# Norm sums in column strips, inverse roots spread by row groups: one change to a hybrid decoder kernel

## The reference

```
z = einsum('btd,dn->btn', h, w_in)                       # one projection, 88 tiles of 128 columns
q = rms_norm(a_q, a_q_norm) * 64 ** -0.5                 # attention, 3 groups x 8 heads x 64
k = rms_norm(a_k, a_k_norm)
o_b = rms_norm(o_b, b_out_norm) * silu(b_g)              # gated linear attention (GLA), 4 heads x 128
cq = l2_norm(cq) * 128 ** -0.5;  ck = l2_norm(ck)        # gated DeltaNet, 4 heads x 128
o_c = rms_norm(o_c, c_out_norm) * silu(c_z)

def rms_norm(x, w): return x * rsqrt(mean(x * x) + 1e-6) * w
def l2_norm(x):     return x * rsqrt(sum(x * x) + 1e-6)
```

## Time and profile before

| | |
|---|---|
| median of 3 runs | 1831.47 us (1829.76 to 1833.31) |
| profiled execution | 1828.83 us, span 1826.8 us |
| TensorE busy | 1749.6 us, 96% |
| VectorE, ScalarE, GpSimd busy | 746.2 (41%), 362.8 (20%), 154.7 us (8%) |
| chain that ended last | PE 85%, DMA 7%, SP's queue 3%, DVE 2% |

### The profile page before, as it was taken

One profiled execution on the slowest core, in us unless ns is written; L12 is line 12 of the kernel. 1 busy time (PEld: TensorE's weight loads), 2 busy tenths in 40 slices (PEclk: granted clock), 3 DMA queues, 4 the chain that ended last, 5 costly groups with the idle time before them and its releaser, 6 DMA issues.

```text
span 1826.8 us, 30009 instructions
## 1 busy us (share of the span) xinstructions
PE 1749.6 (96%) x12509; PEld 1289.6 (71%) x12509; DVE 746.2 (41%) x1549; ACT 362.8 (20%) x760; POOL 154.7 (8%) x259
## 2 busy tenths in 40 slices
PE   8999999999999999999999998999979989999987
PEld 5888888787768999978898887866844343333434
DVE  3444542434536676443635314273243222233222
ACT  2141333323101000013213343231010100100001
POOL 3000000403200111000100001041000000000000
PEclk9999999999999999999999999999989999999999
DMA  9833599999999997899527899899658999999993
GB/s 270 288 121 110 178 326 318 357 318 353 384 348 388 374 324 271 307 352 369 160 77 264 285 349 340 314 375 380 220 209 311 393 378 414 387 398 393 380 415 150
DMA packets 263163, 563.94 MB, mean 309 GB/s; under 512 B 11965, under 2 KB 160673, under 8 KB 262752
## 3 DMA queue, kind: packets, MB, share of 16 engines
q1 hardware_dynamic: 243696, 500.14, 75.8%
q0 software_dynamic: 18544, 58.58, 9.2%
q10 hardware_dynamic: 784, 3.25, 0.5%
HBM read 547.74 MB, written 196.63 MB: 407 GB/s over the span
## 4 chain that ended last, share of the span: by engine, by line
PE 85%; DMA 7%; SPq 3%; DVE 2%; issue 1%; ACT 1%; POOL 0%; ACTq 0%; DVEq 0%; POOLq 0%
PE PS L929 34%; PE PS L1580 7%; PE PS L1361 7%; PE PS L1337 4%; PE PS L1369 4%; PE PS L850 3%; SPq L804 3%; PE PS L1351 3%; PE PS L1618 3%; DMA mem<-in_moe_w_up 3%; PE PS L973 3%; PE PS L1560 3%; DMA z<-in_moe_w_down 2%; PE PS L966 2%; PE PS L1521 2%
## 5 line engine op out<-in xcount | busy, mean ns | idle before, releaser
L929 PE MATMUL PS<-h,mem 128*128 128x264 f32 x2816 | 655.2, 389 | 0.0
L929 PEld LDWEIGHTS PS<-h,mem 128*128 128x128 f32 x2816 | 528.5, 191 | 107.0 <-issue 21.3
L1763 ACT COPY z<-PS 128x264 f32<-128x264 f32 (+6 forms) x311 | 127.6, 431 | 817.3 <-PE PS L929 528.4
L1580 PE MATMUL PS<-mem,z 128*32 128x512 f32 (+1 forms) x1536 | 150.4, 536 | 12.4 <-DMA mem<-in_moe_w_up 5.8
L1580 PEld LDWEIGHTS PS<-mem,z 128*32 128x32 f32 x1536 | 52.9, 113 | 87.4 <-issue 77.1
L2841 DVE COPY small<-mem 128x1024 f32 x56 | 38.9, 694 | 171.8 <-PE PS L1560 109.4
L1560 PE MATMUL PS<-small,z 128*32 128x256 f32 (+2 forms) x624 | 87.8, 396 | 0.0
L1337 PE MATMUL PS<-z,mem 128*128 128x264 f32 x384 | 87.3, 388 | 0.0
L1560 PE MATMUL PS<-z 128*32 128x256 f32 (+2 forms) x624 | 87.0, 396 | 0.0
L1337 PEld LDWEIGHTS PS<-z,mem 128*128 128x128 f32 x384 | 72.3, 190 | 13.8 <-issue 1.7
L1361 PE MATMUL PS<-z,mem 128*128 128x132 f32 x624 | 77.4, 276 | 0.0
(11 more groups left out here) (364 smaller groups left out, 2018.9 us busy)
## 6 DMA issues: line engine op xcount, KB each, us to landing
out_win_s<-in_cache_win_kv SPq DMA_DIRECT2D x128, 1023.5 KB, 11.6
mem<-in_w_in SPq DMA_DIRECT2D x88, 1024.0 KB, 7.4
mem<-in_moe_w_gate SPq DMA_DIRECT2D x40, 1024.0 KB, 12.7
mem<-in_moe_w_up SPq DMA_DIRECT2D x40, 1024.0 KB, 12.6
mem<-in_moe_w_down SPq DMA_DIRECT2D x32, 1024.0 KB, 15.6
out_win_s<-in_cache_win_kv SPq DMA_DIRECT2D x32, 1022.0 KB, 12.4
z<-in_moe_w_down SPq DMA_DIRECT2D x24, 1024.0 KB, 14.2
z<-in_moe_w_up SPq DMA_DIRECT2D x16, 1024.0 KB, 13.7
```

The costliest lines, as they stand in the source:

```text
L929: last = mm(bank(l, "p", j)[:, 0:T], w[:, k, P * (j % 2):P * (j % 2) + P], h[:, k, :], start=(k == 0), stop=(k == KT - 1))
L1580: last = mm(m_bank("c", "gu", g, b, w, r)[BLK * j:BLK * j + BLK, 0:n], hs[:, k, P * r + BLK * j:P * r + BLK * j + BLK], v3(slot_ap(set_slo ...
L1763: return nc.scalar.copy(out, in_)
```

## The change

`norm_sum` on TensorE becomes four products of 32 columns: `K(...)[:, 48:80]`, the 32 columns of the matrix that straddle its middle, against one tile of squares each, written to four strips of 32 partitions of one bank, `n1`. So the sums of tile t lie in rows 32t to 32t + 31; with `blk` the first 16 of them are those of the head's lower half, the others those of the upper. ScalarE takes one logarithm and one exponential over that bank, 264 columns. A new step `norm_out` spreads the result: four products of 32 rows (row group t) with the constant `spread`, which picks row 0 of the group for the output's partitions 0 to 63 and row 16 for the others, into four banks `n4`. VectorE then multiplies each of the four tiles with its bank, out of PSUM, and frees the bank; norms other than 2 and 9 end in a drain that raises `n4_done`. In the list `norm_out` stands one `proj` tile behind its `norm_sum`.

```diff
@@ -40,7 +40,7 @@
 K_NAMES = ["ident", "ones", "blk", "upper", "neg_t", "pos_s", "low16", "bd16", "m32t", "m64t", "m128t", "hmap",
-           "gla", "iota", "hsel", "bsel", "esel", "jsel", "umask", "gmask"]
+           "gla", "iota", "hsel", "bsel", "esel", "jsel", "umask", "gmask", "spread"]
 K_W = dict(hmap=512, hsel=24, bsel=8, esel=64, jsel=4, umask=8, gmask=4)
 K_OFF = {}
 _o = 0
@@ -86,7 +86,7 @@
     for j in range(2, 6):
         s += p(2) + [("conv_v", j)]
     s += [("conv_s",)] + p() + [("conv_t",)] + p() + [("conv_a",)] + p(2) + [("cz",)] + p()
-    s += [("norm_sq", 0)] + p() + [("norm_sum", 0), ("norm_sq", 1)] + p() + [("norm_sum", 1)] + p()
+    s += [("norm_sq", 0)] + p() + [("norm_sum", 0), ("norm_sq", 1)] + p() + [("norm_out", 0), ("norm_sum", 1)] + p() + [("norm_out", 1)]
     def around(*step):
         j = next(proj)
         return [step, ("proj_half", j), (step[0] + "2", *step[1:]), ("proj", j)]
@@ -100,13 +100,13 @@
         s += around("gdn_st", i)
     s += [("gs_a",)] + p() + [("gs_t",), ("gla_x",), ("gla_vb",)] + p() + [("gs_b",), ("gla_b",)] + p()
     s += [("gla_g",), ("gla_e",)] + p() + [("norm_sq", 2)] + p(2) + [("norm_sum", 2), ("gs_c", 0), ("gla_k",)] + p()
-    s += [("gla_a", 0), ("gs_c", 1), ("norm_sq", 3)] + p() + [("gla_o", 0), ("gla_a", 1)] + p()
-    s += [("gs_d",), ("norm_sum", 3), ("gla_o", 1), ("gla_ch", 0)] + p() + [("norm_sq", 4), ("gla_ch", 1)] + p()
-    s += [("norm_sum", 4), ("gla_ch", 2)] + p() + [("norm_sq", 5), ("gla_ch", 3), ("gx_t",)] + p()
-    s += [("norm_sum", 5), ("gx_m",)] + p() + [("gx_u",)] + p(2) + [("gx_q",), ("norm_sq", 6)] + p() + [("gx_r",), ("norm_sum", 6)]
+    s += [("norm_out", 2), ("gla_a", 0), ("gs_c", 1), ("norm_sq", 3)] + p() + [("gla_o", 0), ("gla_a", 1)] + p()
+    s += [("gs_d",), ("norm_sum", 3), ("gla_o", 1), ("gla_ch", 0)] + p() + [("norm_out", 3), ("norm_sq", 4), ("gla_ch", 1)] + p()
+    s += [("norm_sum", 4), ("gla_ch", 2)] + p() + [("norm_out", 4), ("norm_sq", 5), ("gla_ch", 3), ("gx_t",)] + p()
+    s += [("norm_sum", 5), ("gx_m",)] + p() + [("norm_out", 5), ("gx_u",)] + p(2) + [("gx_q",), ("norm_sq", 6)] + p() + [("gx_r",), ("norm_sum", 6)]
     for n in range(7, 10):
-        s += p() + [("norm_sq", n)] + p() + [("norm_sum", n)]
-    s += p()
+        s += p() + [("norm_out", n - 1), ("norm_sq", n)] + p() + [("norm_sum", n)]
+    s += p() + [("norm_out", 9)]
     s += p(64 - 21 - 18 - 16 - 8) + [("kv_tok",), ("att_sc", 0)]
     for t in range(AH // 2):
         s += [("att_sc", t + 1)] * (t + 1 < AH // 2) + p(2) + [("att_pt", t)] + p(2) + [("att_pv", t)]
@@ -140,6 +140,8 @@
     if k == "gate_c":
         return [("btok",)]
     if k == "norm_sum":
+        return [("n1", a[0])]
+    if k == "norm_out":
         return [("n4", a[0], t) for t in range(4)]
     if k == "gdn_dec":
         return [("brow", *a)]
@@ -246,6 +248,7 @@
     for b in (32, 64, 128):
         m = low & (row // b == col // b) & (row // (b // 2) != col // (b // 2))
         put(f"m{b}t", m.T * 1.0)
+    put("spread", ((row % 32 == 0) & (col < 64)) * 1.0 + ((row % 32 == 16) & (col >= 64)) * 1.0)
     put("gla", ((row <= col) & (row // BC == col // BC)) * 1.0)
     put("iota", np.broadcast_to(r, (P, P)))
     bh = np.arange(64)[:, None]
@@ -961,9 +964,18 @@
             def norm_sum(l, n):
                 pe.wait_ge(sems["sq4"], V("sq4", l, n))
+                open_bank(pe, l, "n1", n)
                 for t in range(4):
+                    last = mm(bank(l, "n1", n)[32 * t:32 * t + 32, 0:T], K(N4[n][2])[:, 48:80], sq4(n)[:, t, :],
+                              start=True, stop=True)
+                last.then_inc(full(l, "n1", n), 1)
+
+            def norm_out(l, n):
+                pe.wait_ge(sems["rs4"], V("rs4", l, n))
+                for t in range(4):
+                    rows = slice(32 * t, 32 * t + 32)
                     open_bank(pe, l, "n4", n, t)
-                    mm(bank(l, "n4", n, t)[:, 0:T], K(N4[n][2]), sq4(n)[:, t, :], start=True, stop=True).then_inc(
+                    mm(bank(l, "n4", n, t)[:, 0:T], K("spread")[rows, :], sq4(n)[rows, 0, :], start=True, stop=True).then_inc(
                         full(l, "n4", n, t), 1)
             def heads(job, left, right):
...
@@ -1840,14 +1852,10 @@
                 act_(sq4(n), buf[:, base:base + 4, :], ACT.Square).then_inc(sems["sq4"], 1)
             def norm_sum(l, n):
-                scale = N4[n][3]
-                for t in range(4):
-                    wait_full(act, l, "n4", n, t)
-                    act_(sq4(n)[:, t, :], bank(l, "n4", n, t)[:, 0:T], ACT.Ln, scale=scale, bias=epsc).then_inc(
-                        free(l, "n4", n, t), 1)
-                for t in range(4):
-                    wait_read(act, l, "n4", n, t)
-                act_(sq4(n), sq4(n), ACT.Exp, scale=-0.5).then_inc(sems["rs4"], 1)
+                wait_full(act, l, "n1", n)
+                act_(sq4(n)[:, 0, :], bank(l, "n1", n)[:, 0:T], ACT.Ln, scale=N4[n][3], bias=epsc).then_inc(free(l, "n1", n), 1)
+                wait_read(act, l, "n1", n)
+                act_(sq4(n)[:, 0, :], sq4(n)[:, 0, :], ACT.Exp, scale=-0.5).then_inc(sems["rs4"], 1)
             def gdn_dec(l, i):
                 wait_full(act, l, "brow", i)
@@ -2224,18 +2232,20 @@
                 wait_read(dve, l, "btok")
                 ts(nbtok, btok, -1.0, None, MUL).then_inc(sems["btok_ready"], 1)
-            def norm_sum(l, n):
+            def norm_out(l, n):
                 buf, base, _, _s, w = N4[n]
-                dve.wait_ge(sems["rs4"], V("rs4", l, n))
-                t_ = buf[:, base:base + 4, :]
-                if n < 2:
-                    stt(t_, t_, float(CD) ** -0.5 if n == 0 else 1.0, sq4(n), MUL, MUL).then_inc(sems["n4_done"], 1)
-                elif n in (2, 9):
-                    link(stt(t_, t_, w, sq4(n), MUL, MUL))
+                by = float(CD) ** -0.5 if n == 0 else 1.0 if n == 1 else w
+                for t in range(4):
+                    t_ = buf[:, base + t, :]
+                    wait_full(dve, l, "n4", n, t)
+                    stt(t_, t_, by, bank(l, "n4", n, t)[:, 0:T], MUL, MUL).then_inc(free(l, "n4", n, t), 1)
+                if n in (2, 9):
+                    for t in range(4):
+                        wait_read(dve, l, "n4", n, t)
                     g_ = z[:, Z_CZ:Z_CZ + 4, :] if n == 2 else z[:, Z_BG:Z_BG + 4, :]
-                    tt(g_, g_, t_, MUL).then_inc(sems["n4_done"], 1)
+                    tt(g_, g_, buf[:, base:base + 4, :], MUL).then_inc(sems["n4_done"], 1)
                 else:
-                    stt(t_, t_, w, sq4(n), MUL, MUL).then_inc(sems["n4_done"], 1)
+                    dve.drain().then_inc(sems["n4_done"], 1)
             def gdn_dec(l, i):
                 if i:
...
```

More of the change, by code:

```diff
@@ L1720, in _ @@
             run = dict(params=params, tables=tables, small=small_step, small_turn=small_turn, proj=proj, proj_half=proj_half, conv_s=conv_s, conv_t=conv_t, gate_c=gate_c,
-                       norm_sum=norm_sum, gdn_dec=gdn_dec, gdn_a=gdn_a, gdn_a2=gdn_a2,
+                       norm_sum=norm_sum, norm_out=norm_out, gdn_dec=gdn_dec, gdn_a=gdn_a, gdn_a2=gdn_a2,
                        gdn_lv=gdn_lv, gdn_lv2=gdn_lv2, gdn_st=gdn_st, gdn_st2=gdn_st2,
@@ L2914, in _ @@
             run = dict(small=small_step, small_turn=small_turn, conv_v=conv_v, conv_s=conv_s, conv_t=conv_t, conv_a=conv_a,
-                       cz=cz, gate_c=gate_c, norm_sum=norm_sum, gdn_dec=gdn_dec, gdn_a=gdn_a, gdn_inv=gdn_inv,
+                       cz=cz, gate_c=gate_c, norm_out=norm_out, gdn_dec=gdn_dec, gdn_a=gdn_a, gdn_inv=gdn_inv,
                        gdn_lv=gdn_lv, gdn_st=gdn_st, gs_a=gs_a, gs_t=gs_t, gs_b=gs_b, gs_c=gs_c, gs_d=gs_d, gla_g=gla_g,
```

## The result

The changed kernel takes 1834.97 us (median of 20 runs, 1832.11 to 1837.2). The kernel before, run beside it, takes 1832.3 (20 runs, 1828.18 to 1837.19). The ratio is 1.0017, with a 95% interval of 1.001 to 1.0024: slower by 1.8 to 4.4 us, about 2.7 in the medians. Forecast were 1829.8 us and a difference of -1.7. The range holds the time, and the difference is under the 0.2% that I called the bound of no change, but it has the other sign, and 20 runs of each tell it from zero. Two executions among the experiments ran far longer than all others, one of e3 (3898.9 us) and one of the kernel before beside e5 to e8 (6072.7 us); the ratios leave them out.

The account below looks back on a forecast made before the run. TensorE, holding 85% of the chain, was taken to bound the kernel. The terms -4.1 - 1.5 - 1.0 + 3.7 + 1.2 gave -1.7 us, from 1831.5 to about 1829.8 us, range 1824 to 1837.

Parts of the forecast that it names:

- Products: TensorE's norm products: 1.59 us replaces 1.78 in 20 norms, and some array turns fall away; together -4.1 us.
- second `gs_c`: TensorE at L1077: its reads now come ahead of norm 2's multiplies, loss 0.3 instead of 1.06 us; -1.5 us.
- `gx_u`: TensorE's wait at L1162 goes, but two of its banks are held by norm 5's multiplies; -1.0 us.
- the prices of the turns: TensorE going into tiling mode and back: 0.33 us for the sums in strips, 0.36 for the spreading in row groups.
- rivals C: At the norm products: four times faster by strips alone, no cost of switching mode; 14 us better, 1815.8 us; chance 0.03.
- D: At the norm products: strips or row groups run one after another, 4.25 us per norm; +49 us, 1878; chance 0.01.
- ScalarE: In the norms: one logarithm and exponential over 264 columns frees `proj` banks sooner, but no product waits; nothing gained.
- VectorE: In the norms: one 1.32 us multiply becomes four taking 1.72 us; the length alone costs nothing.
- the delta rule: `gdn_a` waits for norm 1's `n4_done`, now about 2 us behind `norm_out` 1; 1.1 us of cover, so nothing.
- step (4): End of norm 9: bias tables issued 8.8 us after the sums instead of 6.88, lengthening the first score waits; +3.7 us.
- The clock: Around the scores: layer 0's low-clock stretch grows to the length of layer 1's, which stays as it is; +1.2 us.
- Rival A: At the first scores: tables land much later, beside SyncE's load and copies; +6.9 us in all, 1838.4; chance 0.23.

Follow-up runs that it names:

- e3: The changed kernel with norm 9 kept in the old form (four full products, no `proj` tile between): 1825.64 us, 0.9979 of the kernel before.
- e5: The changed kernel itself, unaltered, measured and traced a second time: 1832.75 us, 1.0015 of the kernel before.
- e8: The changed kernel with SyncE's two 1 MB cache copies behind weight chunk 37 instead of 36: 1826.01 us, 0.9982 of the kernel before.
- e7: The kernel before with only the delay: VectorE's multiply of norm 9 waits for the next `proj` tile; 1837.89 us, 1.0048 of the kernel before.
- e11: The kernel before with norm 9's multiply delayed by a `proj` tile and SyncE's two copies one chunk later: 1834.37 us, 1.0025 of the kernel before.
- e10: The kernel before with SyncE's two 1 MB copies one chunk later and nothing else: 1828.33 us, 0.9996 of the kernel before.
- e2: The changed kernel with POOL starting the bias tables when norm 8 is done instead of norm 9: 1820.58 us, 0.9955 of the kernel before.
- e12: Second run of the changed kernel with the bias tables started when norm 8 is done instead of norm 9: 1818.76 us, 0.9951 of the kernel before.
- e1: The kernel before with POOL starting the bias tables when norm 8 is done instead of norm 9: 1829.75 us, 1.0011 of the kernel before.
- e4: The changed kernel with the ten stores of k and v put ahead of the last two bias tables on POOL: 1834.81 us, 1.0028 of the kernel before.

## Why the prediction was wrong, by its own steps

- **Products (-4.1), second `gs_c` (-1.5), `gx_u` (-1.0): right.** Sums 0.78 us as said, spreading 0.86 for 0.81, `gs_c` 1.47 for 1.4, the wait at `gx_u` 1.1 for 0.9. Read at `kv_tok` the three give -6.1 instead of -6.6. Taking the prices of the turns from the transposes and `gs_c` of the kernel before held; rivals C (1815.8) and D (1878; by its own terms the sum gives 1883) are out with it.
- **ScalarE, VectorE, the delta rule at nothing: no row speaks against it.** Four multiplies that read PSUM take 1.69 us (1.72 said), and no new wait of TensorE stands between 80 us and norm 9.
- **The end of norm 9, step (4): the term that failed.** The issue is 8.83 us behind the sums (8.8 said), and the first waits are 3.08 and 5.28 us (2.5 and 4.9 said), 4.6 more than before for 3.7. The waits that follow them in the scores shrank by 1.2, so the view of waits has 11.5 - 8.1 = 3.4, and this part of the term held. What the step had no price for is its last sentence, the ten stores, "a few tenths later than these stores can begin now". They do begin 0.4 us later behind the sums, and take some 4 us longer each to land (median 13.7 for 9.3). VectorE's second batch of scores waits for one of them, and TensorE gets a wait of 3.1 us in all at L853 that the kernel before doesn't have. I counted when the stores are issued and took their landing as given.
- **The clock (+1.2): too small.** Layer 0's stretch grew to 6.8 us, as said; a further 3.4 came in each layer, 10.2 us more at low clock in all, for which 3.4 had been put down at +1.2. At the same rate that is 3.6. Two pairs of traces with the same TensorE instructions are near this rate: up to the product of the router (L1478), e7 is 7.8 us later than the kernel before with 4.8 more of waits, e11 5.9 with 1.4, each with 10.2 us more at low clock. That leaves 3.0 and 4.5.
- **The sum.** Step (4) and the clock were +4.9 together. e7 measures +8.8 for this delay (6.2 to 11.3). With the -6.1 read from the trace that gives +2.7, and 2.7 was measured; with so wide an interval the fit to a tenth is luck. From the trace it is 3.4 + 3.1 + 3.6 = 10.1, less 1.0 for the cache wait that is gone.
- **Rival A had the place and the sign, and half of the mechanism.** It counted SyncE's load and two copies at 8.8 us behind the sums, the same instant as the tables, and I then argued it away with "the tables are on POOL's queue and SyncE's is not ahead of them there". The transfers don't meet in a queue; e8 and e11 show that they delay each other all the same. Where I was off in A too: the tables' median landing grows only from 9.1 to 10.1 us, and none takes longer than 12.4. It is the stores behind them that grow.
- **The extra 4 us or so in the traces.** Behind the scores the trace after has low stretches at 571.8 (6.8 us) and 1203.3 (3.4 us) that the trace before lacks. The changed kernel's second trace (e5) has them too. But near 570 every other trace read here has one of 3.4 or 6.8 us, also those of kernels that are no slower than the one before (e10 at 569.5, e2 at 565.5): the trace of the kernel before, 3.5 us under its median, is the exception. What sets these stretches isn't settled; the medians don't depend on one trace.

What stays open: e1 gains nothing where e2 gains 11 us with the same edit. Most of this is that the kernel before had less to gain: its waits at the scores and behind are 8.1 us against 11.5 + 3.1, and the edit brings them to 5.9 + 1.7 and 5.5 + 1.1. The waits of e1 add to -2.2 + 1.7 + 0.6, no gain. Its wait at L850 lies in layer 0, where VectorE waits 7.57 us for a store; why that store lands so late while the median is 8.0 us I have not tested. e4's median is well above what its trace's waits and the norms sum to. Nor is it tested what SyncE's 1 MB load, which no run moved, costs beside the tables. And the clock was never isolated: no run holds the waits and changes the clock alone, so the 3.6 us put on it is an estimate from these traces, not measured.

## What to carry to other kernels

When a step is moved, follow not only its signal to the next waiting instruction but also the transfers it releases, through to their landing and to who waits for that landing. Ask what the other queues issue in the same microsecond: here the stores behind tables that started 2.2 us ahead of another queue's 3 MB landed after 9.3 us in the median, and after 13.7 when both started together. And if a transfer's buffers come free earlier than the signal it waits for, try the earlier signal; here that turned a change of +0.17% into one of -0.5%, and in the kernel before it gained nothing.

## What the runs showed of the hardware

- Stores issued on one queue behind four 384 KB tables landed after a median of 9.3 us while another queue's 3 MB began 2.2 us behind the tables, after 13.7 with both beginning together, and after 9.8 with 2 of these 3 MB moved away to 355.59 (e8). e7 and e11 repeat it in the other kernel: 13.8 and 9.9.
- Four fp32 products of 32 rows by 264 columns in four row groups (eight records) took 0.66 us in the chain, four of 32 output columns in four column strips 0.58, and the 16 `proj` records behind either set 3.76 instead of 3.56.
- A `SCALAR_TENSOR_TENSOR` of 128 x 264 fp32 with one input in PSUM took 0.48 us each (481 to 490 ns over 48); four in a row took 1.69, no more than the 1.72 without it.
- Stretches of low clock came or stayed away in traces of one and the same kernel with the same waits before them: with TensorE's waits of 0.59 and 2.16 us in layer 1's scores, e12 ran 6.8 us at a granted 0.50 from 1097.1 and e2 none there. So one trace alone doesn't price a change of a few microseconds here.
